# The low weight parts made by GpSimd in two halves with a signal each, and one FFN unit's high part moved behind the first sigmoid

## The reference

```
p = rmsnorm(x) @ w_in                            # first block
x = x + concat(y_rwkv, y_attn) @ w_out;  x = rmsnorm(x)
proj = rmsnorm(x) @ w_in_2                       # mixer
k, vm = split(rmsnorm(mem) @ w_kv_2)             # 256 memory tokens
merged = g0 * (a @ w_a_out) + g1 * (b @ w_b_out) + g2 * (c @ w_att_out)
x = x + merged @ w_o_2
gt, up = split(causal_dwconv(rmsnorm(x) @ w_up_2, conv_ffn_w))   # FFN
x = x + (silu(gt) * up) @ w_down_2;  out = rmsnorm(x)
```

## Time and profile before

| what | us |
|---|---|
| median of 3 runs (lowest, highest) | 1459.35 (1457.43, 1460.45) |
| the profiled execution, its own time | 1459.89 |
| its span in the profile | 1458.1 |
| TensorE matmuls busy | 1408.7 (97%) |
| VectorE busy | 929.3 (64%) |
| ScalarE, GpSimd busy | 494.8, 492.3 (34% each) |

### The profile page before, as it was taken

How to read it: one execution, slowest core, us unless ns; L and a number is a source line. 1 busy time by engine, 2 the same in 40 slices (tenths; PEclk the granted TensorE clock), 3 DMA queues, 4 the chain that set the end, 5 groups by cost and what they waited for, 6 DMA issues and landing times.

```text
span 1458.1 us, 18647 instructions
## 1 busy us (share of the span) xinstructions
PE 1408.7 (97%) x7612; PEld 1147.9 (79%) x7612; DVE 929.3 (64%) x1327; ACT 494.8 (34%) x679; POOL 492.3 (34%) x139
## 2 busy tenths in 40 slices
PE   7999988899998999999999999999998999999998
PEld 6778656788888877888888887878886888888886
DVE  6679977535413357769969974772358888885122
ACT  5443475443324232122222223322234333332121
POOL 0003210112535323433434433334433343443441
PEclk9999999799999999999999999999999999999999
DMA  6221000203324211222222231223222223222221
GB/s 207 87 87 58 30 2 1 78 17 113 124 77 145 87 58 59 87 105 98 87 105 97 87 115 58 87 91 112 87 87 74 100 87 116 87 89 106 81 100 58
DMA packets 21349, 125.14 MB, mean 86 GB/s; under 512 B 2384, under 2 KB 3408, under 8 KB 7696
## 3 DMA queue, kind: packets, MB, share of 16 engines
q1 hardware_dynamic: 20752, 121.71, 23.2%
q10 hardware_dynamic: 512, 2.23, 0.4%
HBM read 121.84 MB, written 2.10 MB: 85 GB/s over the span
## 4 chain that ended last, share of the span: by engine, by line
PE 83%; DVE 11%; ACT 3%; issue 2%; DMA 1%; SPq 0%; DVEq 0%; ACTq 0%
PE bank L411 23%; PE bank L412 23%; PE bank L413 23%; DVE score L1989 2%; DVE misc L1988 2%; PE bank L362 1%; PE bank L1029 1%; PE bank L1045 1%; DVE conv_b L2490 1%; PE bank L680 1%; DMA x_res<-in_x 1%; ACT prob L1464 1%; PE bank L402 1%; PE bank L897 1%; DVE op_lo L1815 1%
## 5 line engine op out<-in xcount | busy, mean ns | idle before, releaser
L1240 POOL TENSOR_TENSOR w_lo<-w_raw,w_hi 128x2048 fp32r<-128x2048 f32 (+1 forms) x102 | 468.2, 4590 | 753.2 <-ACT w_hi L1304 737.3
L411 PE MATMUL bank<-op_hi,w_hi 128*128 128x512 f32 x1312 | 515.8, 393 | 10.2 <-issue 6.6
L413 PE MATMUL bank<-op_hi,w_lo 128*128 128x512 f32 x1312 | 511.7, 390 | 0.0
L412 PE MATMUL bank<-op_lo,w_hi 128*128 128x512 f32 x1312 | 511.6, 390 | 0.0
L411 PEld LDWEIGHTS bank<-op_hi,w_hi 128*128 128x128 f32 x1312 | 246.9, 188 | 65.5 <-issue 10.2
L1304 ACT ACTIVATE w_hi<-w_raw 128x2048 fp32r<-128x2048 f32 (+2 forms) x109 | 205.6, 1887 | 263.1 <-PE bank L413 263.1
L412 PEld LDWEIGHTS bank<-op_lo,w_hi 128*128 128x128 f32 x1312 | 246.9, 188 | 51.4 <-issue 0.7
L413 PEld LDWEIGHTS bank<-op_hi,w_lo 128*128 128x128 f32 x1312 | 246.8, 188 | 51.3
L2383 DVE SCALAR_TENSOR_TENSOR bank<-pad_b,par,bank 128x512 f32<-128x512 f32 x232 | 175.3, 756 | 7.8
L2280 DVE TENSOR_TENSOR x_res<-bank,x_res 128x512 f32<-128x512 f32 x24 | 16.5, 691 | 129.0 <-PE bank L413 129.0
L2560 DVE TENSOR_TENSOR tmp<-tmp,conv_f 128x512 f32<-128x512 f32 x22 | 88.4, 4019 | 13.3 <-ACT tmp L1760 13.3
(11 more groups left out here) (394 smaller groups left out, 1796.5 us busy)
## 6 DMA issues: line engine op xcount, KB each, us to landing
w_raw<-in_w_units SPq DMA_DIRECT2D x104, 1024.0 KB, 4.8
w_raw<-in_w_units SPq DMA_DIRECT2D x4, 768.0 KB, 4.1
x_res<-in_x SPq DMA_DIRECT2D x8, 256.0 KB, 6.8
x_res<-in_x ACTq DMA_DIRECT2D x2, 1024.0 KB, 7.0
out<-x_res SPq DMA_DIRECT2D x8, 256.0 KB, 2.1
w_raw<-in_w_units SPq DMA_DIRECT2D x3, 512.0 KB, 9.6
w_raw<-in_w_units SPq DMA_DIRECT2D x4, 256.0 KB, 5.6
mem_tok<-in_mem SPq DMA_DIRECT2D x1, 1024.0 KB, 4.8
```

The source lines that it names most:

```text
L411: nc.tensor.matmul(b[:, 0:width], h, xh[:, x0 + k, 0:width], start=start and k == ks[0], stop=False)
L412: nc.tensor.matmul(b[:, 0:width], h, xl(x0 + k, width), start=False, stop=False)
L413: mm = nc.tensor.matmul(b[:, 0:width], l, xh[:, x0 + k, 0:width], start=False, stop=stop and k == ks[-1])
L1240: nc.gpsimd.tensor_tensor(w_lo[u % 2][:, 0:nk, :], w_raw[u % 2][:, 0:nk, :], w_hi[u % 2][:, 0:nk, :].bitcast(F32), ALU.subtract).then_inc( ...
```

## The change

There are two edits.

POOL's split_lo makes the low part of a unit in two instructions, chunks 0 to 3 and chunks 4 to 7 (4 and 5 in a unit of 6 chunks), and each counts lo_ready. lo_count(u, halves) tells what the count is once the first, or both halves, of unit u are there. TensorE's next_unit waits for the first half; tile, and the loop of the vm units, wait for both before chunk 4. SP and POOL themselves wait for both halves of the unit they waited for before.

On ACT the high part of the fifth up unit (i = 4) is made behind the sigmoid of unit 0, where it stood behind the taps of unit 2; the sixth stands behind the taps of unit 2, where it stood behind those of unit 3; from the seventh on the places are the same.

```diff
+        def lo_count(u, halves=2):
+            return min(u + 1, FIRST_POOL_UNIT) + max(0, 2 * (u - FIRST_POOL_UNIT) + halves)
...
                 pe.wait_ge(hi_ready, u + 1)
-                pe.wait_ge(lo_ready, u + 1)
+                pe.wait_ge(lo_ready, lo_count(u, 1))
...
                 for k in ks:
+                    if k == CH // 2 and u >= FIRST_POOL_UNIT:
+                        pe.wait_ge(lo_ready, lo_count(u))
...
                     for k in range(CH):
+                        if k == CH // 2:
+                            pe.wait_ge(lo_ready, lo_count(u))
...
                 sp.wait_ge(hi_ready, u - 1)
-                sp.wait_ge(lo_ready, u - 1)
+                sp.wait_ge(lo_ready, lo_count(u - 2))
...
-                pool.wait_ge(lo_ready, u)
-                nc.gpsimd.tensor_tensor(w_lo[u % 2][:, 0:nk, :], w_raw[u % 2][:, 0:nk, :],
-                                        w_hi[u % 2][:, 0:nk, :].bitcast(F32), ALU.subtract).then_inc(lo_ready, 1)
+                pool.wait_ge(lo_ready, lo_count(u - 1))
+                for ks in (slice(0, CH // 2), slice(CH // 2, nk)):
+                    nc.gpsimd.tensor_tensor(w_lo[u % 2][:, ks, :], w_raw[u % 2][:, ks, :],
+                                            w_hi[u % 2][:, ks, :].bitcast(F32), ALU.subtract).then_inc(lo_ready, 1)
...
-                if i >= PLAIN_UNITS:
+                if i == PLAIN_UNITS or i > PLAIN_UNITS + 1:
                     after_unit()
                 evacuated(act, ("up", i, 0))
                 A(sig_f[i % 2][:, 0:T], conv_f[i % 2][0][:, 0:T], ACT.Sigmoid).then_inc(sem("cg_sig"), 1)
+                if i == 0:
+                    after_unit()
```

More of the change, by code:

```diff
@@ L1175, in _ @@
             sp.wait_ge(hi_ready, first_phase2_unit - 1)
-            sp.wait_ge(lo_ready, first_phase2_unit - 1)
+            sp.wait_ge(lo_ready, lo_count(first_phase2_unit - 2))
             filled(sp, ("ga", 0, 1))
```

## The result

| | us |
|---|---|
| kernel before, median of 4 executions (lowest, highest) | 1459.11 (1457.43, 1460.45) |
| changed kernel, median of 4 (lowest, highest) | 1439.78 (1437.12, 1446.28) |
| ratio, with its 95% interval | 0.9875 (0.984 to 0.9909) |
| changed kernel, the profiled execution, its own time and its span | 1439.87 and 1438.1 |

The prediction said 1449.4, within 1445.5 to 1453.5. The sign and the places were right, the size was not.

The account below looks back on a forecast made before the run. TensorE, computing 97% of the span, was taken as the bound, with stalls on POOL's low part to remove. Gains 7.8 + 2.7 + 0 + 0 + 0 = 10.5 us, from 1459.89 to 1449.4, range 1445.5 to 1453.5.

Parts of the forecast that it names:

- up units 3 and 4: FFN start: stalls waiting for POOL's low part go, with some 2.1 us at the lower clock; 7.8 us, lower end 4.
- kT 2 and u 0: kT stretch: stalls before these two units go as the first half comes earlier; 2.7 us, ends 1.4 and 2.8.
- vm 3 to wout 1: Mixing stage: VectorE's last op_lo ends it, so an earlier vm start brings 0, range -0.5 to +2.1 us.
- mixer to y(1,0): At 958.26: TensorE still waits for VectorE's op_lo held by POOL; gain 0, ends -0.3 and +1 us.
- the port rule: kT stretch: VectorE slips in between POOL's halves, delaying the second signal up to 0.7 us; sum could be 1.4 smaller.
- Rival 3: Chunk 4 of every tile: added waits stop weight loads running ahead, 203 times; at 0.08 us each, 1465.6 us; chance 0.05.
- Rival 5: Early signal doesn't release TensorE before the second, only the moved split works; gain 7.2, 1452.7 us; chance 0.03.
- Rival 1: Up units 3 and 4 freed, halves bring little elsewhere, kT keeps most of its stall; 1451.6 us; chance 0.10.
- rival 2: Up unit 6's split late behind VectorE's chain: 1.9 us stall plus up to 2 of lower clock; 1453.3 us; chance 0.10.
- narrow place: Up unit 6: split follows VectorE-bound taps; first half at 1142.7 against 1143.2 wanted, holding with 0.5 us.
- rival 4: Vm 1.5, y 1, first stage 1: shorter holds on VectorE help there too; gain 14, 1445.9 us; chance 0.08.
- the term for the clock: Up units 3 and 4: some 2.1 us of work at the lower clock around the stall, gone without the stall.

Follow-up runs that it names:

- Early halves: Kernel before with only the four units POOL makes early (units 9 to 12) in halves: 1459.49 us, ratio 1.0011.
- its equivalents: Kernel before with only units 9 to 12 in halves, 1459.49 us; kernel before with only 203 always-met waits at chunk 4 added, 1459.32 us.
- the new place alone: Kernel before with only ACT's high part moved behind the first FFN sigmoid, POOL's instruction whole: 1452.72 us, second batch 1453.07 us.
- the padded kernel: Kernel before with six superfluous full matmuls ahead of the small token-sum matmuls in up unit 0: 1458.63 us, ratio 1.0002.
- quarters and the order of wout 0: Changed kernel with POOL's low part in four pieces and wout 0's chunks 4 to 7 made first: 1438.51 us, second batch 1442.44 us.

## Why the prediction was wrong

The prediction's terms beside the profiled pair. Each gain is the difference of how far apart the same matmuls lie in the two traces; the second and third numbers are its parts in full-clock and lost time.

| place | predicted | measured | full-clock | lost |
|---|---|---|---|---|
| up units 3 and 4 | 7.8 | 7.8 | 4.4 | 3.4 |
| kT 2 and u 0 | 2.7 | 2.75 | 2.75 | 0 |
| vm 3 to wout 1 | 0 (-0.5 to +2.1) | 1.1 | 1.1 | 0 |
| mixer to y(1,0) | 0 (-0.3 to +1) | -0.8 | 0.9 | -1.7 |
| up unit 0 | none | 1.6 | -0.1 | 1.7 |
| before 360 us | none | 6.8 | 0 | 6.8 |
| sum | 10.5 | 19.2 | 9.0 | 10.2 |

The spans differ by 19.9 before rounding; the 0.7 left are in the last 14 us, where the split does not hold (above), and are not in the table.

**What held.** Units 3 and 4: 7.8 predicted, 7.8 measured, the part of the clock with it. I booked 5.07 of stall and 2.1 at the clock; in the table's terms, where idling at the lower clock counts half, they are 4.4 and 3.4 with unit 3. kT: 2.7 and 2.75. The 1.4 us that could go there by the port rule did not: POOL's pairs in the kT units took 4.78 us, as long as undisturbed, and VectorE's steps read a bank. ACT's high part stands behind the sigmoid, POOL's halves are there in number, met waits are free. Rival 3, the slower one, needed 0.052 us a wait and got 0.0005 (error 0.0025). Rival 5 needed the early signal to do nothing, and it is worth over 3 us. Rival 1 had the kT units keep their stall, and it is gone; rival 2 had up unit 6 late, and it is not. One size was off: a half takes 2.40 us undisturbed and 2.49 on average, where I had 2.35, which cost nothing.

**Unit 6 was no narrow place.** I had 0.5 us of slack, from VectorE's chain laid out late. In the trace its high part starts at 1122.96 and the pair of 1124.95 is whole at 1129.83, for a start 10.88 behind 1120.87, at 1131.75: 1.9 us even for the whole. My layout had set VectorE's chain back by a whole low part, up to 4.7 us; between 1097 and 1141 us no VectorE instruction lasts longer than 2.9.

**The smaller terms, each low.** vm and wout 0 gave 1.1 where I took 0. vm 3 starts 1.6 us earlier, wout 0 gives 1.3 back, as foreseen, since it needs both halves; then the wait for the mixing operand goes. At y(1,0) I wrote that the total stays at 2.7. VectorE's chunk 5 is ready at 948.1, and TensorE waits 1.79 instead of 2.38. It waits once only, and for chunk 5, not for 4:

```profile
942.74 2.62 DVE L1825 CAST op_hi<-conv_b 128x512 fp32r<-128x512 f32 x1
945.39 2.74 DVE L1826 TENSOR_TENSOR op_lo<-conv_b,op_hi 128x512 fp32r<-128x512 f32 x1
948.05 0.41 DVE L1825 CAST op_hi<-conv_b 128x512 fp32r<-128x512 f32 x1
948.50 0.69 DVE L1826 TENSOR_TENSOR op_lo<-conv_b,op_hi 128x512 fp32r<-128x512 f32 x1
```

POOL's pair there runs from 942.26 for 5.31. Of the eight op_lo steps the one at 945.39 is the sixth, so the copy of chunk 5 is held by the first half and its subtraction by the second. Chunk 4's subtraction began at 942.12, just before POOL, and was not held. I had laid the holds on chunks 4 and 5, with POOL and VectorE in the same places to each other as in the earlier trace rows; with the changes ahead they had shifted by one VectorE step, and chunk 5 is due later than chunk 4. These two places are 1.1 and 0.9 us of full-clock time, 2.0 together. This is where rival 4 was right in its mechanism: shorter holds of VectorE alone are worth some 1.6 us. I gave it 8 in 100, and the time it named, 1445.9, was still 6 us too high.

**The step that failed: the term for the clock.** In the paragraph on up units 3 and 4 I took 2.1 us as all that the clock gives, and the sum subtracts from one profiled execution as if the rest of its low stretches would stand. In the counting of the table the sum held 7.1 us of full-clock time and 3.4 of lost time. Over many executions the change gives 9.9 and 6.6. So the miss is 2.8 us of full-clock time, of which the two places above show 2.0, and 3.2 (1.0) of lost time. Set against means, the forecast is 1457.7 - 10.5 = 1447.2, the measured mean 1441.2, and the 6.0 between them are these two. The 0.8 that no place shows is mostly the end, where the split counts it wrongly; by the traces without the end the stalls gave 9.0, so they were 1.9 short, and an estimated 4.1 of the 6.0 is the clock.

**And the range.** Lost time is anywhere from 20 to 31 us in executions of the kernel before, and from 13 to 25 of the changed one. The medians shown had narrow bounds (1457.43 to 1460.45), yet 109 executions reach from 1451.5 to 1461.1. The medians of the result (1459.11 and 1439.78) lie 1.4 us above and 1.4 below the means of all executions, so 2.8 of their 19.3 us are chance in four executions each. My range took in only terms of stalls, and nothing for this.

**What stays open.** Why lost time falls by 3.2 us (4.1 by the estimate above) beyond unit 4. Early halves don't do it (26.3 us lost with them alone). In the traces most of the difference lies before 360 us: 17.1 to 20.5 us lost there in the kernel before and its equivalents, 8.5 to 12.0 in the changed one. But both traces with the new place alone have 10.2 there as well, and their code is the old one up to 1111 us. The long stretch at 284 us comes and goes between executions; if early halves make it rarer, that is a further part, for which the counts are too few. The fall in up unit 0, 1.7 us, is the one place at which all eight traces with halves agree, and the padded kernel speaks for the moment at which the small matmuls come. The rest, 1.5 us (2.4 by the estimate), I can't place, and its error is 1.0.

## What to carry to other kernels

Split every execution in full-clock time and time lost to the clock, and sum stalls only against the first; leave out the end, where TensorE has nothing to do. Ten executions settle the first to half a microsecond, while the second needs many more. A variation of several us in the clock belongs in the range even where the few times shown lie close together. When POOL and VectorE both read SBUF, cutting POOL's long instruction in two helps twice: here the early signal gave some 3.5 us and VectorE's shorter waits some 1.6.

## What the runs showed of the hardware

- Two POOL instructions without a wait between them let a VectorE instruction through. VectorE's hold fell from 4.93 us to at most 2.9, and the pair took 5.2 us where it took 4.75 undisturbed. A one-input copy of VectorE was held as well (942.74, 2.62 us, where the same copy takes 0.41).
- 203 met semaphore waits in the middle of TensorE's work cost nothing (ratio 1.0013, 1.0 to 1.0026; full-clock time the same to 0.1 us, with an error of 0.5).
- The time at the 1.2 GHz level is not fixed by the program: with the same code the stretch at 284 us lasted 13.7 us in one execution and 3.4 in another, and the kernel before lost 20 to 31 us to the clock over 109 executions.
- Less stall did not show as less time: 4.5 us of full-clock time won with quarters and the order of wout 0 gave a mean only 1.0 us lower, with an error of 1.6.
